# Routed experts: five chunks of every expert's weights land in places of their own, and GpSimd copies them for each block

## What is computed

```python
logits = xt @ w_router + b_router                  # 256 tokens, 32 experts
top_v, top_e = lax.top_k(logits, 4)
gates = softmax(top_v)
# for each token t and each of its four experts e:
hgu  = h[t] @ w1[e] + b1[e]                        # 1024 -> 2048 (gate, up)
act  = min(gate, 7) * sigmoid(1.702 * min(gate, 7)) * (clip(up, -7, 7) + 1)
y[t] += gates[t, e] * (act @ w2[e] + b2[e])        # 1024 -> 1024
out = rms_norm(x + gate2 * y, final_norm_w)
```

## Time and profile before

| | |
|---|---|
| median of 3 runs | 2311.32 us (2311.12 to 2313.72) |
| profiled execution | 2313.27 us, its span 2311.5 us |
| TensorE busy | 2186.8 us (95%) |
| VectorE busy | 1360.3 us (59%) |
| ScalarE busy | 622.2 us (27%) |
| GpSimd busy | 101.7 us (4%) |
| data moved | 569.59 MB, mean 246 GB/s |

### The profile page before, as it was taken

How to read it: one execution, slowest core, us unless ns; L and a number is a source line. 1 busy time by engine, 2 the same in 40 slices (tenths; PEclk the granted TensorE clock), 3 DMA queues, 4 the chain that set the end, 5 groups by cost and what they waited for, 6 DMA issues and landing times. The chain is left out here.

```text
span 2311.5 us, 53432 instructions
## 1 busy us (share of the span) xinstructions
PE 2186.8 (95%) x22199; PEld 1398.5 (61%) x22200; DVE 1360.3 (59%) x2861; ACT 622.2 (27%) x1591; POOL 101.7 (4%) x234
## 2 busy tenths in 40 slices
PE   8999899999999999999999899899899889989987
PEld 3546685478744578777878656466456446645644
DVE  4989468453895663636745464555465555646455
ACT  3018442443221363336343311111111111111112
POOL 0001000000000051002001000000000000000000
PEclk9999999999999999999999999999999999999999
DMA  9670035301477103331240699989989998998997
GB/s 400 247 290 34 1 146 191 110 1 43 176 267 277 39 2 109 110 110 38 74 160 24 237 401 419 421 348 421 421 364 421 421 421 364 421 422 367 421 421 297
DMA packets 109778, 569.59 MB, mean 246 GB/s; under 512 B 11600, under 2 KB 13136, under 8 KB 50928
## 3 DMA queue, kind: packets, MB, share of 16 engines
q1 hardware_dynamic: 109680, 568.28, 61.4%
HBM read 567.19 MB, written 1.05 MB: 246 GB/s over the span
## 5 line engine op out<-in xcount | busy, mean ns | idle before, releaser
L3061 PE MATMUL PS<-BIG,PW 128*32 128x256 f32 x9216 | 527.2, 381 | 53.6 <-DMA BIG<-in_w 48.0
L3061 PEld LDWEIGHTS PS<-BIG,PW 128*32 128x32 f32 x9216 | 292.8, 110 | 286.0 <-DMA BIG<-in_w 102.7
L3097 PE MATMUL PS<-BIG,PW 128*32 128x256 f32 x4608 | 255.5, 379 | 0.0
L3310 DVE TENSOR_SCALAR PW<-PS 128x512 f32<-128x512 f32 x36 | 24.9, 692 | 337.9 <-PE PS L3061 337.9
L3097 PEld LDWEIGHTS PS<-BIG,PW 128*32 128x32 f32 x4608 | 149.6, 110 | 99.2 <-DVE PW L3319 0.4
L2921 ACT ACTIVATE PW<-PW 128x512 f32<-128x512 f32 x36 | 22.7, 630 | 672.3 <-DVE PW L3310 671.9
L386 DVE SCALAR_TENSOR_TENSOR BIG<-BIG,COND_ROWS 128x1024 f32<-128x1024 f32 x128 | 153.3, 1220 | 24.2 <-DMA BIG<-in_w_ada_columns 23.9
L1148 PE MATMUL PS<-HT,BIG 128*128 128x512 f32 (+1 forms) x448 | 152.0, 501 | 0.0
L2909 ACT ACTIVATE PW<-BIG,MOD,GAIN 128x64 f32<-128x64 f32 x296 | 102.2, 428 | 160.4 <-DVE BIG L3236 160.4
L1148 PEld LDWEIGHTS PS<-HT,BIG 128*128 128x128 f32 x448 | 85.1, 190 | 65.3 <-issue 60.3
L3325 DVE SCALAR_TENSOR_TENSOR HT<-HT,SM 128x1024 f32<-128x1024 f32 x72 | 91.6, 1273 | 45.9 <-DMA BIG<-in_b_rows 44.6
(11 more groups left out here) (544 smaller groups left out, 3185.8 us busy)
## 6 DMA issues: line engine op xcount, KB each, us to landing
BIG<-in_w SPq DMA_DIRECT2D x384, 1024.0 KB, 20.0
BIG<-in_l_w_ada_columns SPq DMA_DIRECT2D x40, 1024.0 KB, 7.2
BIG<-in_l_w_in SPq DMA_DIRECT2D x19, 2048.0 KB, 8.0
BIG<-in_w_ada_columns SPq DMA_DIRECT2D x24, 1024.0 KB, 7.0
BIG<-in_l_w_out SPq DMA_DIRECT2D x8, 2048.0 KB, 8.4
BIG<-in_w_in SPq DMA_DIRECT2D x7, 2048.0 KB, 7.9
BIG<-in_l_w_ada SPq DMA_DIRECT2D x4, 2048.0 KB, 18.2
BIG<-in_w_out SPq DMA_DIRECT2D x2, 2048.0 KB, 7.8
```

The costliest lines, as they stand in the source:

```text
L3061: ins = nc.tensor.matmul(part_of(4 + half, g, u).rearrange("p (k x) -> p k x", x=64), xt[:, u, c, :], columns[:, :, g, :], start=False, st ...
L3097: ins = nc.tensor.matmul(part_of(7, g, u), at_[:, u, k, :], W[:, 8 + k // 2, k % 2 * D + g * 256:k % 2 * D + g * 256 + 256], start=(k == 0 ...
```

## The change

Chunks 0 to 4 of every expert are no longer loaded into their places in `W`, but into five places of their own (`staged`, in `BIG` behind the 12). GpSimd copies each of the five from there into `W`, for every block, also for the second block of an expert. A copy waits for the chunk to have landed and for TensorE to have used the place in the block before; it counts on `chunk_copied`, which TensorE waits for in place of the landing. SyncE loads a staged chunk of the next expert as soon as it has been copied for the last block of the present one. In the program of SyncE the bias row's load now stands behind those five loads, and `norm_rows` behind all of expert 1, with a wait for the scaled `bias2`. Eleven chunks of expert 0, in place of eight, are loaded ahead of `done[7]`. Small tables move out of `BIG` into `CONST`, `COND_ROWS` and the new `LAST_ROWS`.

```diff
+        STAGED = 5
+        staged = BIG[:, 12 * 2048:(12 + STAGED) * 2048].rearrange("p (c n) -> p c n", c=STAGED)
         def load_expert_chunk(sp, e, c):
+            dst = staged[:, c, :] if c < STAGED else expert_weights[:, c, :]
...
-        early_chunks = [2 * free_slot, 2 * free_slot + 1, *range(6, 12)]
+        early_chunks = [*range(STAGED), *(c for c in range(STAGED, 12) if c >= 6 or c // 2 == free_slot)]
...
                     sp.dma_start(bias2[0:E, :], t["b2_2"]).then_inc(S["late_loaded"].sem, 16)
-                    sp.dma_start(norm_rows, t["final_norm_w_2"].partition_broadcast(P)).then_inc(S["late_loaded"].sem, 16)
+
+                    def load_behind(last, e, row):
+
+                        for c in range(STAGED):
+                            sp.wait_ge(loop["chunk_copied"], last * STAGED + (c + 1))
+                            load_expert_chunk(sp, e, c)
+                        sp.wait_ge(loop["bias_used"], last + 1)
+                        load_bias1(sp, row)
+                        for c in range(STAGED, 12):
+                            sp.wait_ge(used, last * 12 + (c + 1))
+                            load_expert_chunk(sp, e, c)
 
                     sp.wait_ge(loop["first_blocks_ready"], 1)
                     last = sp.value_load(first_blocks[0:1, :], min_val=0, max_val=LAT // SLOT - 1)
-                    sp.wait_ge(loop["bias_used"], last + 1)
-                    load_bias1(sp, slice(1, 2))
-                    for c in range(12):
-                        sp.wait_ge(used, last * 12 + (c + 1))
-                        load_expert_chunk(sp, 1, c)
+                    load_behind(last, 1, slice(1, 2))
+                    sp.wait_ge(loop["bias2_scaled"], 1)
+                    sp.dma_start(norm_rows, t["final_norm_w_2"].partition_broadcast(P)).then_inc(S["late_loaded"].sem, 16)
...
-                        sp.wait_ge(loop["bias_used"], last + 1)
-                        load_bias1(sp, bass.ds(e, 1))
-                        for c in range(12):
-                            sp.wait_ge(used, last * 12 + (c + 1))
-                            load_expert_chunk(sp, e, c)
+                        load_behind(last, e, bass.ds(e, 1))
...
+                @block.gpsimd
+                def _(pool):
+                    passed = SM[:, 704:704 + STAGED]
+
+                    def copy_staged(c):
+                        nc.gpsimd.tensor_copy(W[:, c, :], staged[:, c, :]).then_inc(loop["chunk_copied"], 1)
+
+                    pool.wait_ge(*done[7])
+                    for c in range(STAGED):
+                        pool.wait_ge(chunk_landed[c], 16)
+                        copy_staged(c)
+                    n = trips(pool)
+                    with pool.Fori(1, n) as i:
+                        load = pool.value_load(plan[0:1, bass.ds(i, 1)], min_val=0, max_val=E - 1)
+                        for c in range(STAGED):
+                            pool.wait_ge(chunk_landed[c], load * 16 + 16)
+                            pool.wait_ge(used, i * 12 + (c - 11))
+                            nc.gpsimd.tensor_tensor(passed[:, c:c + 1], ones[:, 0:1], ones[:, 0:1], ALU.add)
+                            copy_staged(c)
...
-                            pe.wait_ge(chunk_landed[c], load * 16 + 16)
+                            if c < STAGED:
+                                pe.wait_ge(loop["chunk_copied"], i * STAGED + (c + 1))
+                            else:
+                                pe.wait_ge(chunk_landed[c], load * 16 + 16)
```

More of the change, by code:

```diff
@@ L189, in layers_and_experts_kernel @@
         SM = sb("SM", [P, 720])
-        ST = sb("ST", [P, 64])
+        LAST_ROWS = sb("LAST_ROWS", [P, D])
+        ST = LAST_ROWS[:, 0:64]
         ring = BIG[:, 0:RING_N].rearrange("p (s n) -> p s n", s=SLOTS)
@@ L2052, in layers_and_experts_kernel @@
         window_layer(3, False)
+        STAGED = 5
         expert_weights = BIG[:, 0:12 * 2048].rearrange("p (c n) -> p c n", c=12)
+        staged = BIG[:, 12 * 2048:(12 + STAGED) * 2048].rearrange("p (c n) -> p c n", c=STAGED)
         chunk_landed = [ctx.enter_context(nc.semaphore(f"expert_chunk{c}_landed")) for c in range(12)]
         def load_expert_chunk(sp, e, c):
+            dst = staged[:, c, :] if c < STAGED else expert_weights[:, c, :]
             if c < 8:
-                src, dst = t["w1_2"].rearrange("e d f -> (e d) f")[bass.ds(e * D + c * P, P), :], expert_weights[:, c, :]
+                src = t["w1_2"].rearrange("e d f -> (e d) f")[bass.ds(e * D + c * P, P), :]
             else:
                 src = t["w2_2"].rearrange("e f d -> (e f) d")[bass.ds(e * D + (c - 8) * 2 * P, 2 * P), :].rearrange("(p j) n -> p (j n)", p=P)
-                dst = expert_weights[:, c, :]
             sp.dma_start(dst, src).then_inc(chunk_landed[c], 16)
         free_slot = (ws.first["w_out_2"] + 2) % SLOTS
-        early_chunks = [2 * free_slot, 2 * free_slot + 1, *range(6, 12)]
-        w_router = BIG[:, 12 * 2048:12 * 2048 + KT * 32].rearrange("p (k e) -> p k e", k=KT)
+        early_chunks = [*range(STAGED), *(c for c in range(STAGED, 12) if c >= 6 or c // 2 == free_slot)]
+        masks_at = consts_at["cos"][0]
+        w_router = CONST[:, masks_at:masks_at + KT * 32].rearrange("p (k e) -> p k e", k=KT)
         token_rms, token_rstd = SM[:, 700:702], SM[:, 702:704]
@@ L2767, in take @@
                                                              **dict(zip(names, shape)))
[L2769 to L2774, removed]
-            gates_of, dest0, gates_known = by_token[:, :, 0:E], by_token[:, :, E:E + K], by_token[:, :, E + K:E + 2 * K]
[L2776 to L2780, removed]
+            masks, more_masks, rows = [masks_at + KT * E], [consts_at["causal"][0]], [0]
+            cond_rows = COND_ROWS[:].rearrange("p r d -> p (r d)")
+            htok, bias2 = take(cond_rows, rows, 2, D), take(cond_rows, rows, D)
+            bias1, scores_by = take(CONST, masks, 256), take(CONST, masks, LAT)
+            onehot, placed = take(CONST, masks, 2, K, E), take(CONST, masks, 2, K, E)
+            gates_by = take(CONST, masks, LAT)
+            assert masks[0] <= consts_at["upto"][0]
+            xturned = take(CONST, more_masks, 2, KT, PART)
+            gain_split, by_token = take(CONST, more_masks, 256), take(CONST, more_masks, 2, E + 2 * K)
+            assert more_masks[0] <= consts_at["slot_row"][0]
+            gates_of, dest0, gates_known = by_token[:, :, 0:E], by_token[:, :, E:E + K], by_token[:, :, E + K:E + 2 * K]
+            gain_rows = norm_rows = LAST_ROWS[:]
             pw = [0]
@@ L2821, in routed_experts @@
                 "y_copied scattered bias_used ranked order_ready plan_ready plan_turned plan_copied gate_exp_ready gates_ready gates_spread "
[L2822 removed]
+                "last_rows_ready gains_copied first_blocks_ready places_ready places_copied gates_turned gates_copied chunk_copied bias2_scaled bias2_added gather_turned xt_copied "
                 "router_scaled shift_summed squares_gathered".split())}
@@ L3358, in _ @@
                     tables(lambda x: 10 + x)
-                    dve.wait_ge(*at("late_loaded", 32))
+                    dve.wait_ge(*at("late_loaded", 16))
                     nc.vector.tensor_tensor(bias2[0:E, :], bias2[0:E, :], gain_rows[0:E, :], ALU.mult).then_inc(loop["bias2_scaled"], 1)
@@ L3391, in scale_half @@
                             ending["half_normed"], 1)
+                    dve.wait_ge(*at("late_loaded", 32))
                     dve.wait_ge(ending["tiles_scattered"], 1)
```

1 line of the change is left out of this document (removed).

## The result

The changed kernel takes **2366.96 us** in the median of four runs (2361.62 to 2371.71), the kernel before 2312.45 beside it: a ratio of 1.0235, 95% interval 1.0211 to 1.0260. It is slower by 54.5 us. The forecast was 2354, with a range of 2320 to 2376. The profiled execution took 2371.71 us, its span 2369.9.

The account below looks back on a forecast made before the run. The prediction took the stream of weights as the bound. Its terms, 8 + 5.8 + 7.5 + 22 = +43 on the profiled 2313.3, gave 2356.6, forecast as 2354 us since the median stood 2.0 lower; range 2320 to 2376.

Parts of the forecast that it names:

- rival C: GpSimd's copies are slow, near 4.1 us each, holding routing, `activation` and TensorE at chunk 4: 2372 us, chance 0.15.
- The order of the queue: Weight loads: one queue in order, so the bias row lands 10.0 us after chunk 0 instead of 3.0 before.
- Rival A: Bias row gets past the queued chunks in time, copies hidden, norm's gain costing nothing: faster, 2303 us, chance 0.10.
- Bias waits of some 8 us per one-block expert, over 200 in all: Sign of being right: VectorE's wait for bias rows goes from 44.6 us to over 200.
- Term 3, the end: Last block, held by the late bias row, ends 37.6 us after its chunk 0 lands, before 30.1: +7.5 us.
- Term 3, the stops: At two-block experts each stop of the weight stream is 13.4 us instead of 7.9: 4 x 5.5 = +22 us.
- no block starts before T + 12.9: Each block starts at earliest 12.9 us after chunk 0 lands: bias row at 10.0, then 2.9 to TensorE's start.
- + 37.6: At a two-block expert the second block starts 37.6 us after chunk 0 lands, the first block taking 24.7 us.
- Term 1: Start of the stage: GpSimd's copies delay VectorE's routing by 5 us and block 1 by 3: +8 us.
- Term 2: SyncE waits for scaled `bias2` to load the norm's gain, so expert 2's chunk 0 lands later: +5.8 us.
- Term 4: Copies in the steady stream, 2.4 us each, delay nothing, as the block starts later anyway: 0.
- Rival B: Bias row is in time, but delays from copies against the routing and the norm's gain stand: 2317 us, chance 0.08.

Follow-up runs that it names:

- experiment 1: The changed kernel with only the bias row's load put back ahead of the five staged chunks: 2321.92 us.
- experiment 2: The kernel before, without staging or copies, with the bias row's load moved behind chunk 4: 2360.78 us for 2313.41.
- experiment 3: The changed kernel with the bias row's load behind chunk 2, then behind chunk 1: 2343.32 and 2333.68 us.
- experiment 4: The changed kernel with all GpSimd copies cut to 32 columns, then only chunk 4's copy cut: 2354.78 and 2356.78 us.
- experiment 5: The changed kernel with the load of the final norm's gain, and its wait, behind all experts: 2361.60 us.

## Why the prediction was right, and where not

- *The total.* The way and the mechanism were right, the size was short: 43 us slower by the forecast, 54.5 measured. The forecast's own bounds ended at 2364 (and its terms, added up, give 2338 to 2362, not 2342 to 2364). The measured 2367 lies in the range because the range had taken in rival C, whose slow copies did not come; that part is luck.
- *The order of the queue.* Right. The row lands 0.1 us behind chunk 4, at T + 10; experiments 1 and 2 put 45 and 47 us on its place alone. Rival A, the row that gets past the megabytes, had nothing for it.
- *Bias waits of some 8 us per one-block expert, over 200 in all*: 134.7 in 26, so 5.2 us each. I left out that behind a later block VectorE itself comes later to the row (1513.46 - 5.16 = T + 4.9 in the block above).
- *Term 3, the end*: +7.7 for +7.5, but by luck. In the last block VectorE's operation was not held and took 1.28 us, and the products took 14.02. In the two kernels of experiment 3 and the one with chunk 4's copy cut, the last block had one of the two or both, and ended at T + 33.6, 36.2 and 39.4, where 30.1, 32.6 and 37.6 were in the forecast's terms.
- *Term 3, the stops*, is **the term that was mis-sized**: 13.4 us a stop forecast, 16.3 measured in the mean and 17.0 in the block above; +22 in all, with bounds of +8 and +30, and +34 measured. The mechanism held, chunk 5 waiting for a second block that starts late. Two sizes in "no block starts before T + 12.9" and "+ 37.6" were wrong: the 2.9 us from the row to TensorE's start became 4.6, since the copy of chunk 4 lands on `gates_of_slots` (experiment 4), and the 24.7 us of the first block became 26.4, since its products ran at a lower clock after the wait (experiment 2 has it without copies). Together 3.4 of the 3.6 us of that block; without the two, stops of 12.8 to 13.1 us were left. The forecast had the first in its hands: the earlier trace rows were used for the routing, and the steady stream was priced at 0 with a look at `activation` only. By the rule of the Trainium skill, SBUF — State Buffer, "Who interferes with whom" (an operation of VectorE with two SBUF inputs and a GpSimd one that reads SBUF exclude each other, whichever issues first), up to 1.7 us a stop were to be had. The trace agrees in both directions, 3.02 us for 1.28 at 1513.46, and a copy of 2.96 us at 2326.02 beside an unheld 1.28 at 2325.95; in both cases the recorded start of VectorE's operation is 0.05 to 0.07 us ahead of the copy's, so the records don't show which went first.
- *Term 1*: +4.6 for +8. The copy was taken at 2.4 us and took 1.89 when nothing held it (1.97 in the mean). Its 5 us on the routing stood; the 3 for block 1 did not. By the Trainium skill, GPSIMD Engine Reference, "Engine selection" (work with one input runs roughly at line rate), the prediction had an estimated 1.7 us, nearer than the 2.4 that I took.
- *Term 2*: +6.0 for +5.8, and 5.0 in the trace of experiment 5. The forecast's two ends were both off a little: chunk 0 of expert 2 had landed at 1366.5 and not 1367.7, for the stream paused by 1.4 us behind expert 3 and was not continuous, and from issue to landing it took 4.9 us and not 5.6.
- *Term 4*, the copies in the steady stream: 0 was right where the row is in time (experiment 1), and up to 1.7 us a stop where it is late.
- *Rival B*, with its stop of 5.8 us and 2317 us, is what experiment 1 ran: 5.6 to 6.8 us by the single landings, 2321.9 us. Its kernel holds the five staged chunks behind the row, and the row waits for the second block's `lay_bias`: the next chunk 0 lands at T + 33.2, and chunk 5 goes out at T + 41.7.
- *Rival C*, slow copies: no, 1.97 us.

## What to carry to other kernels

A few kilobytes that an engine needs first belong ahead of the megabytes in an ordered queue: here behind the first two megabytes each further one cost 2.6 to 3.0 us at every two-block expert, 45 us in all with five ahead. Before staging transfers to hide a stop, follow the first one that has no second place: with five of twelve staged, and the row too, the stop moved to chunk 5 and shrank from 7.7 us to 5.6, no further. And a copy that "costs nothing" on an idle engine has to be laid against each operation beside it that reads two inputs from SBUF, at the moment it will run, above all the one that everyone has just begun to wait for. It is not only those: a cast and a TENSOR_SCALAR with one input were held here as well (1.18 us for 0.17, 1.80 for 0.18).

## What was unexpected

TensorE's granted clock fell after short idle times. In the changed kernel first products took 15.3 to 16.8 us in 14 of the 17 blocks that began after 3.19 to 8.04 us without work, and 14.02 us after all six waits of up to 1.72 us (in experiment 2 they took 15.5 us already after 2.36 to 2.39 us); its mean clock over the span is 0.975 for 0.992 before. One of the 14, after the 6.7 us at 1488.14:

```profile
1488.14 15.37 PE L3091 MATMUL PS<-BIG,PW 128*32 128x256 f32 x256 [6.74 <-DVE PS L3207]
```

So a wait that TensorE could have afforded (a block needs 24.7 of 29.9 us) has a second price of up to 2.8 us, and it falls on the path wherever a second block follows. A version that keeps TensorE busy through the wait was not tried.
